# Attention's blocks in the order q, k, z, v, with probabilities turned through memory

## The reference, cut to what matters

```
h = RMSNorm(x);  proj = h @ w_in
attention:  12 heads x 128, three dilated windows mixed:
            s = q k^T / sqrt(128) + log_count      (log_count: -1e30 where no window holds the pair)
            p = exp(s - max s);  o = (p v / sum p) * silu(z)
conv:       o = b * conv3(c * u) * silu(z)         retention: o = norm(decayed (q k^T) v) * silu(z)
merged = sum over the branches of sigmoid(g) * (o @ w_branch)
x = x + RMSNorm(merged @ w_out)
```

## Time and profile before

| | |
|---|---|
| median of 3 runs | 2713.33 us (2712.95 to 2714.37) |
| the profiled execution's own time | 2712.87 us |
| its span (first to last instruction) | 2711.0 us |
| TensorE busy | 2699.1 us, 12120 matmuls |
| VectorE busy | 1881.8 us |
| ScalarE busy | 1308.4 us |
| mean granted TensorE clock | 0.999 |
| DMA | 579.43 MB, mean 214 GB/s |
| L1269 on VectorE (`w_trail`) | 1045 x 1223 ns = 1265.2 us |
| L1002 on ScalarE (`w_lead`) | 1045 x 1060 ns = 1101.7 us |
| L1566 on VectorE (turn of the probabilities) | 96 x 569 ns = 54.6 us |

### The profile page before, as it was taken

How to read it: one execution, slowest core, us unless ns; L and a number is a source line. 1 busy time by engine, 2 the same in 40 slices (tenths; PEclk the granted TensorE clock), 3 DMA queues, 4 the chain that set the end, 5 groups by cost and what they waited for, 6 DMA issues and landing times.

```text
span 2711.0 us, 30218 instructions
## 1 busy us (share of the span) xinstructions
PE 2699.1 (100%) x12120; PEld 2240.9 (83%) x12120; DVE 1881.8 (69%) x2102; ACT 1308.4 (48%) x1504; POOL 29.4 (1%) x42
## 2 busy tenths in 40 slices
PE   9999999999999999999999999999999999999998
PEld 7888888888888888888878888888888888888887
DVE  6656775888865666678576567658888656666884
ACT  6454554555543344454454545545555433444543
POOL 0000000000000000000000000000000000000000
PEclk9999999999999999999999999999999999999999
DMA  9677466665666676656576674657656656766563
GB/s 333 212 226 232 163 229 198 230 203 192 228 233 197 206 241 209 217 207 222 178 235 206 217 241 155 235 185 233 226 189 221 234 191 215 233 214 218 202 222 120
DMA packets 299291, 579.43 MB, mean 214 GB/s; under 512 B 12304, under 2 KB 37264, under 8 KB 298896
## 3 DMA queue, kind: packets, MB, share of 16 engines
q1 hardware_dynamic: 260976, 517.50, 56.9%
q10 hardware_dynamic: 37168, 55.13, 7.0%
q0 software_dynamic: 1008, 4.87, 0.5%
HBM read 548.10 MB, written 29.36 MB: 213 GB/s over the span
## 4 chain that ended last, share of the span: by engine, by line
PE 98%; DMA 1%; SPq 1%; DVE 0%; ACT 0%; issue 0%; POOL 0%; DVEq 0%; POOLq 0%
PE ps L928 29%; PE ps L930 29%; PE ps L929 29%; PE ps L895 3%; PE ps L894 3%; PE ps L893 3%; DMA raw<-w_in 0%; SPq L734 0%; PE ps L839 0%; PE ps L837 0%; PE ps L836 0%; PE ps L815 0%; PE ps L819 0%; DMA merged<-xT 0%; PE ps L801 0%; PE ps L820 0%
## 5 line engine op out<-in xcount | busy, mean ns | idle before, releaser
L1269 DVE TENSOR_TENSOR w_trail<-raw,w_lead 128x1024 fp32r<-128x1024 f32 x1045 | 1265.2, 1223 | 770.4 <-ACT w_lead L1002 767.3
L1002 ACT ACTIVATE w_lead<-raw 128x1024 fp32r<-128x1024 f32 x1045 | 1101.7, 1060 | 1250.0 <-PE ps L930 1120.7
L928 PE MATMUL ps<-w_lead,hT_lead 128*128 128x512 f32 x2944 | 1149.4, 390 | 2.1 <-DVE w_trail L1612 1.0
L930 PE MATMUL ps<-w_lead,hT_trail 128*128 128x512 f32 x2944 | 1145.6, 389 | 0.0
L929 PE MATMUL ps<-w_trail,hT_lead 128*128 128x512 f32 x2944 | 1145.5, 389 | 0.0
L928 PEld LDWEIGHTS ps<-w_lead,hT_lead 128*128 128x128 f32 x2944 | 552.7, 188 | 118.1 <-issue 3.6
L930 PEld LDWEIGHTS ps<-w_lead,hT_trail 128*128 128x128 f32 x2944 | 552.6, 188 | 115.0
L929 PEld LDWEIGHTS ps<-w_trail,hT_lead 128*128 128x128 f32 x2944 | 552.8, 188 | 113.5
L928 PE MATMUL ps<-w_lead,oT_lead 128*128 128x512 f32 x576 | 224.2, 389 | 0.0
L930 PE MATMUL ps<-w_lead,oT_trail 128*128 128x512 f32 x576 | 224.1, 389 | 0.0
L929 PE MATMUL ps<-w_trail,oT_lead 128*128 128x512 f32 x576 | 224.1, 389 | 0.0
(11 more groups left out here) (130 smaller groups left out, 1158.9 us busy)
## 6 DMA issues: line engine op xcount, KB each, us to landing
raw<-w_in SPq DMA_DIRECT2D x381, 1024.0 KB, 5.2
raw<-w_out SPq DMA_DIRECT2D x32, 1024.0 KB, 5.1
raw<-w_branch_a SPq DMA_DIRECT2D x24, 1024.0 KB, 5.2
raw<-w_branch_c SPq DMA_DIRECT2D x24, 1024.0 KB, 5.2
raw<-w_branch_r SPq DMA_DIRECT2D x24, 1024.0 KB, 5.4
bounce_q<-vq_sb ACTq DMA_DIRECT2D x18, 512.0 KB, 3.5
vq_sb<-bounce_q ACTq DMA_DIRECT2D x72, 128.0 KB, 4.1
bounce_z<-z_sb ACTq DMA_DIRECT2D x18, 512.0 KB, 4.0
```

What stands on the lines that cost most here:

```text
L928: pe.matmul(acc, lead[:, k, tok(t)], wl, start=opens, stop=False)
L930: last = pe.matmul(acc, trail[:, k, tok(t)], wl, start=False, stop=closes)
L1002: act.activation(w_lead[:, (l * HALVES + h) % SPLIT_SLOTS, :], raw[:, SLOT_OF[l, i][0], part:part + HALF * COLS], ACT.Copy).then_inc(lead_ ...
L1269: dve.tensor_tensor(w_trail[:, s, :], raw[:, SLOT_OF[l, i][0], part:part + HALF * COLS], w_lead[:, s, :].bitcast(F32), ALU.subtract).then_ ...
```

## The change

The order of attention's blocks becomes q, k, z, v. The places in the tables are now counted from attention's third block of a group (z, half 16 of the group). The table entries of attention, in halves from the group's start, are:

| step | before | after |
|---|---|---|
| q, k away (index) | 19, 27 | 18, 20 |
| q, k back (index) | 21, 29 | 20, 22 |
| q, k turned on VectorE (index) | 24, 32 | 23, 24 |
| scores on TensorE (after half) | 32 | 21 |
| scores on VectorE (index) | 36 | 25 |
| exp (index) | 37 | 26, in two parts |
| z leaves the accumulator (index) | 35 | 27 |
| probabilities | turned from index 39 in six pieces | away at 26, back at 29 and 30, turned at 31 and 32 |
| values on TensorE (after half) | 43 | 37 |
| z away, back, turned (index) | 48, 52, 58 | 42, 44, 47 |
| out, ScalarE and VectorE (index) | 59, 59 | 47, 48 |

`exp` writes its result into the tile `gates` (free at that time), already cut into quarters, in two parts of two heads; each part (384 KB) goes to HBM with one DMA and comes back with four, on ScalarE's queue, and VectorE turns it with two transposes of 128x384. The maxima are taken for two heads at a time. `PAIRS` stays as it was, so the branches for paired q and k (`q_scale`, `k_scale`, `scaled`) do nothing. In the diff:

```
-ROLES = {"attention": "vqkz", ...
+ROLES = {"attention": "qkzv", ...
+COUNTED_FROM = {"attention": 2, "conv": 0, "retention": 0}
 PE_DUE:
-    "attention": [("scores", 4 * B), ("values", 5 * B + 3)],
+    "attention": [("scores", 5), ("values", 2 * B + 4.5)],
 ACT_DUE:
-    "attention": [("q_away", 2 * B - 1), ("q_back", 2 * B + 1), ("k_away", 3 * B - 1), ("k_back", 3 * B + 1),
-                  ("exp", 4 * B + 1), ("z_away", 5 * B + 4), ("z_back", 6 * B + 4), ("out", 6 * B + 6.5)],
+    "attention": [("q_scale", -2), ("q_away", -2), ("q_back", 0), ("k_scale", 0), ("k_away", 0), ("k_back", 2),
+                  ("exp0", 6), ("p0_away", 6), ("exp1", 6), ("p1_away", 6), ("p0_back", 9), ("p1_back", 10),
+                  ("z_away", 2 * B + 6), ("z_back", 2 * B + 8), ("out", 2 * B + 11)],
 DVE_DUE:
-    "attention": [("q", 2 * B + 4), ("k", 3 * B + 4), ("scores", 4 * B), ("sums", 4 * B + 2)]
-                 + pieces("probs", 4 * B + 3) + [("values", 5 * B + 3), ("z", 6 * B + 6), ("out", 6 * B + 7)],
+    "attention": [("q", 3), ("k", 4), ("scores", 5), ("sums", 7), ("p0", 11), ("p1", 12),
+                  ("values", 2 * B + 4.5), ("z", 2 * B + 10.5), ("out", 2 * B + 12)],
...
-VALUES_LATE = 4      (v's block no longer leaves four halves late)
...
+        spare = gates[:, 0, 0:HPB * 3 * P].rearrange("p (s c) -> p s c", s=2)
...
+                if what in ("p0", "p1"):
+                    part = int(what[1])
+                    act.wait_ge(exp_ready, HPB * (l * GROUPS + g) + HPB // 2 * (part + 1))
+                    act.dma_start(bounce[what], spare[:, part]).then_inc(away[what], 16)
...
+                elif what in ("exp0", "exp1"):
...
+                    act.wait_ge(neg_max_ready, 2 * (l * GROUPS + g) + part + 1)
+                    by_quarter = spare[:, part].rearrange("p (j h c a) -> p h c j a", j=QUADS, h=HPB // 2, c=3)
...
-            def turn(l, what, mixer, g, piece):
-                src, dst, done = probs, probsT, probs_turned
-                for n in range(a, b):          (16 transposes of 32x384, in six pieces)
+            def turn(l, what, mixer, g):
+                dve.wait_ge(back[what], 16 * QUADS * trips(l, what, mixer, g))
+                squares = spare[:, part].rearrange("p (i h c a) -> p h c i a", i=QUADS, h=HPB // 2, c=3)
+                for h in range(HPB // 2):
+                    last = dve.transpose(probsT[:, HPB // 2 * part + h, :].rearrange("p (c i b) -> p c i b", c=3, i=QUADS),
+                                         squares[:, h])
```

More of the change, by code:

```diff
@@ L500, in build @@
         conv_joined = sem("conv_joined")
-        away = {what: sem(what + "_away") for what in ("q", "k", "z")}
-        back = {what: sem(what + "_back") for what in ("q", "k", "z")}
+        away = {what: sem(what + "_away") for what in ("q", "k", "z", "p0", "p1")}
+        back = {what: sem(what + "_back") for what in ("q", "k", "z", "p0", "p1")}
+        q_scaled = sem("q_scaled")
+        k_scaled = sem("k_scaled")
         q_turned = sem("q_turned")
@@ L1120, in side_work @@
                     bring_back(l, what[:-5], mixer, g)
[L1121 to L1124, removed]
+                elif what in ("q_scale", "k_scale"):
+                    n = role_block(mixer, what[0], g)
+                    if n in PAIR_OF:
+                        tile, done = {"q": (q_sb, q_scaled), "k": (k_sb, k_scaled)}[what[0]]
+                        act.wait_ge(*moved_out(l, n))
+                        for t in range(TILES):
+                            act.activation(quads(tile, t), quads(tile, t), ACT.Copy,
+                                           scale=x_rstd[:, t:t + 1]).then_inc(done, 1)
+                elif what in ("exp0", "exp1"):
+                    part = int(what[-1])
+                    if l > 0 and g == 0 and part == 0:
+                        act.wait_ge(residual_out, l * (16 * OUT_BLOCKS))
+                    act.wait_ge(neg_max_ready, 2 * (l * GROUPS + g) + part + 1)
+                    by_quarter = spare[:, part].rearrange("p (j h c a) -> p h c j a", j=QUADS, h=HPB // 2, c=3)
+                    for h in range(HPB // 2 * part, HPB // 2 * (part + 1)):
+                        for t, tiles in ((0, slice(0, 1)), (1, slice(1, 3))):
                             c = TILES * h + t
-                            last = act.activation(probs[:, h, cols], probs[:, h, cols], ACT.Exp,
+                            taken = probs[:, h, tiles.start * P:tiles.stop * P]
+                            last = act.activation(by_quarter[:, h % (HPB // 2), tiles],
+                                                  taken.rearrange("p (c j a) -> p c j a", j=QUADS, a=SQ), ACT.Exp,
                                                   bias=neg_max[:, c:c + 1], accum_out=row_sum[:, c:c + 1])
@@ L1434, in side_work @@
                         dve.wait_ge(*step_ready(l, s))
[L1435 to L1438, removed]
+                        if mixer != "attention":
                             dve.tensor_tensor(probsT[:, h, :], side(l, s)[:, 0:3 * P], const("causal"),
                                               ALU.mult).then_inc(drained[bank_no(l, s)], 1)
[L1441 to L1447, removed]
+                            continue
+                        dve.scalar_tensor_tensor(probs[:, h, :], side(l, s)[:, 0:3 * P], P ** -0.5,
+                                                 const("log_count"), ALU.mult, ALU.add).then_inc(drained[bank_no(l, s)], 1)
+                        if h % 2:
+                            two = slice(h - 1, h + 1)
+                            for i in range(h - 1, h + 1):
+                                dve.wait_ge(*step_drained(l, STEP["scores", mixer, g, i]))
+                            by_tile = neg_max.rearrange("p (h t) -> p h t", t=TILES)
+                            dve.tensor_reduce(by_tile[:, two, 0], probs[:, two, 0:P], AX_X, ALU.max, negate=True)
+                            dve.tensor_reduce(by_tile[:, two, 1], probs[:, two, P:3 * P], AX_X, ALU.max,
+                                              negate=True).then_inc(neg_max_ready, 1)
                 elif what == "sums":
```

71 lines of the change are left out of this document (38 added, 33 removed).

## The result

| | before | after |
|---|---|---|
| median | 2713.58 us (4 runs) | 2756.8 us (4 runs, 2755.43 to 2759.82) |
| ratio | | 1.0161, 95% interval 1.0143 to 1.0178 |
| span of the profiled execution | 2711.0 us | 2755.9 us |
| mean granted TensorE clock | 0.999 | 0.991 |

The account below looks back on a forecast made before the run. TensorE, 98% of the chain, was taken as the bound. k's turn and trip 15.3 us plus exp beside z 1.2 us made 16.5 us on 2712.87, 2729.4, as a median 2729.8 us; range 2719 to 2744.

Parts of the forecast that it names:

- What bounds the kernel, and where the wait would appear: TensorE bounds the kernel, its busy time stays at 2699 us, and a gap appears ahead of the scores in six groups.
- The bare turn: Before the scores, TensorE waits 1.30 us for k's turn in each of six groups: 7.8 us; as sole-cost rival, 0.15.
- The trip of k: Before the scores, k's late DMAs push its turn; waits including the bare turn: 7.6 + 4.7 + 3.0 = 15.3 us.
- clock of index 24: Time scale in us with 0 at ScalarE's split at index 24; scores wanted at 2.24, k's turn ending at 3.54 at best.
- the late landing, -1.7: Second and third groups, before k's reads: k away lands at most 7.1 us after issue, at -1.7 on the clock of index 24.
- the trips decide: Rival, before the scores: k away lands at the late bound, 24.4 us plus 6 for exp and z, 30.4 us, 2743.7; chance 0.12.
- the -6.0: Second and third groups: k away alone lands in 2.8 us, at -6.0 on the clock of index 24.
- The clock: Rival: TensorE's clock falls after waits, first groups only at risk, some 8 us on top, 2738; chance 0.09.
- sign of being wrong: For the whole kernel, the prediction would be wrong if the granted clock is below 0.99.
- Exp beside z: At indices 26 to 28, exp ahead of z leaves a tenth of cover: 0.2 us x 6 = 1.2 us, bounds 0 and 6.
- Edits at nothing: VectorE's fewer turns, the probabilities' trip, z's turn with out, and v's and the values' places: zero, together within 2 us.

Follow-up runs that it names:

- scores later: The changed kernel with the scores and all that follows up to the turn of the probabilities four halves later: 2714.2 us, ratio 1.0007.
- trip alone: The kernel before with old block order and places, but exp in two parts and the probabilities turned through memory in two parts: 2713.29 us, ratio 1.0002.
- k ahead of q's reads: The changed kernel with k away issued before q back on ScalarE's queue, both still at index 20: 2743.53 us, ratio 1.0115.
- only q's trip earlier: The changed kernel with q away at 17 and back at 19, k staying at 20 and 22: 2745.52 us, ratio 1.0123.
- filled gap: The changed kernel with matmuls whose results nobody reads put ahead of the wait for q's and k's turn before the scores: 2744.05 us, ratio 1.0114.
- scores one half later: The changed kernel with the scores and all that follows up to the turn of the probabilities one half later: 2739.49 us, ratio 1.0098.
- all trips earlier: The changed kernel with q away at 17, k away then q back at 19, k back at 21: 2724.14 us, ratio 1.0042.
- both one index on: The changed kernel with q away 18, back 20, k away 21, back 23, one index later than in only q's trip earlier: 2771.28 us (1 run).

## Why the prediction was wrong, step by step

- **What bounds the kernel, and where the wait would appear.** Right in the place, not in the size. TensorE was the bound, and all six waits that matter stand ahead of the scores. That TensorE's busy time would stay at 2699 was wrong: it was 2716.0, by the clock (below). VectorE's 42.2 us less (41 were forecast) brought nothing in three kernels (after, scores later, trip alone).
- **The bare turn.** Forecast 1.30 us a group. With the trips out of the way four groups have 1.17 or 1.18; the six together 8.1 for 7.8. Right.
- **The trip of k: the step that failed.** Its term with the bare turn was 15.3 us, measured 29.1. The second and third groups were given 1.9 us each (bounds 1.3 and 3.1) and waited 4.02, 3.85, 3.96 and 4.97; the first groups were given 4.7 and 3.0 (late bounds 7 and 5) and waited 6.99 and 5.32. The issue times were right: the send was to be issued by -8.8 on the clock of index 24, whose time 0 would have been 169.12 - 2.72 + 0.48 = 166.9, and it was issued at 158.16 - 166.9 = -8.7. Two things were wrong.
  - The landing of the send. Some 4.4 us was taken, as for q's reads, with 2.8 and 7.1 named as bounds; it took 7.4 to 7.6 us in the second and third groups and 6.0 and 6.1 in the first. The 2.8 of the earlier trace rows is a median over attention and retention: retention's six sends of k took 2.6 us, attention's own 2.9 to 3.5. And the late landing, -1.7, was named but never carried on: the 3.1 us come from a send seen at -4.5 and slow reads (7.1 us), and the rival "the trips decide" takes 3.1 x 4 for the late bound all the same.
  - The path. I had only the reads' landing in the sum of these groups. What ended last was the chain behind the wait on ScalarE's queue: the reads' issue, a split, a trail, q's turn, a trail, k's turn. I had written that chain for the first group of layer 0 alone. With a landing after 7.1 us it gives 3.9 us a group (-1.7 + 1.8 + 1.1 + 1.1 + 1.3 + 1.2 + 1.3 - 2.24). In the second group the scores' weights were wanted at 169.1 and the chain ended at 173.27. By the reads alone, there at 170.8 (3.9 on that clock), the wait would have been 3.0 us. So of the 2.1 us that this group's wait was over 1.9, about 1.1 are the send's late landing, net of reads that were faster than the 6.0 us taken, and 1.0 the chain. This division is read from the trace; no run takes the splits out from behind the reads.
- **The Trainium skill's rule that forbade the -6.0.** I had it in the text (the Trainium skill, DMA: Bandwidth & Descriptors, section Queues, rings and completion order: a completion signal lands only behind the earlier writes of the same DMA engine, whatever queue they came from) and said that the sum was the same with or without it. In after the order was as it says: the last of q's reads landed 6.3 us after the send's issue, the send after 7.4. By the runs the delay comes from loads on another queue too: in the kernel with k ahead of q's reads the send issued 0.39 us behind a load landed at 157.1, the load itself 7.0 us after 149.80, at 156.8. That agrees with the rule. But in the kernel with only q's trip earlier the send was seen at 162.3 and the load issued 0.39 us ahead of it at 163.1, so a send does not wait for the whole of such a load.
- **The clock.** This rival had 0.09 and 8 us, with "nothing" for waits under 3 us. It came in all six groups and cost 12.75 us by the filled gap (15.5 by the counting of starts). The mistake was to give it a chance of its own: it hangs on the length of the gap, so each microsecond of the trips' error moved it too, and with it all six groups were at risk and not the first ones only. Half of the time waited, the rival's rule for the size, gives 14.6 us for the gaps as measured, near the total, but not group by group: 2.75 us more behind 6.99, 2.69 behind 3.85. The rival "the trips decide" (30.4 us) together with the measured 12.75 would be 43, but by luck: of its 30.4 us 6 are for exp and z, which cost nothing, and 24.4 for the trips, which cost 29.1. As a sign of being wrong, a mean clock below 0.99 was too coarse: it was 0.991.
- **Exp beside z.** 1.2 us forecast, 0 measured: no gap at half 27 or 28. The working was close. On the clock of index 26 (split at 181.80, second group of after) split 27 started at 7.0 (7.0 forecast), z was done at 11.4 (11.4), and half 28's trail, started at 193.40, was done at 12.8 (13.0 for its split); TensorE came to half 28 at 195.14, 13.3 (13.1). Some 0.5 us of cover were left, where a tenth was worked out. In the kernel with the scores one half later exp and z's eviction meet at one index, and five groups lose 1.3 us each.
- **Edits at nothing.** Nothing, by two runs (2714.2 with the change but for the scores' place, 2713.29 with the probabilities' trip alone; their intervals reach 4.3 and 3.0 us). Their reads took 5.3 us to land and ended 2.0 us of VectorE's idle time.

## What to carry to other kernels

A transfer's price is that of its place: read what was issued just ahead of it on every queue and has not landed, and if no row shows such a case, carry the loaded bound through the whole sum. When an engine's queue waits for a transfer, carry the delay through everything queued behind it before the next step, not only through the transfer. And price a wait of TensorE together with the clock: here a wait up to 2.3 us cost only itself, and one from 3.8 us on 1.5 to 2.75 us more.

## What the runs showed of the hardware

How long TensorE was idle ahead of the scores, and what its next work took (first score to second matmul behind the scores, 2.93 us at full clock), over 30 gaps of five kernels (after, k ahead of q's reads, scores one half later, all trips earlier, only q's trip earlier):

| gap | clock stayed | clock fell | extra time when it fell |
|---|---|---|---|
| 1.1 to 2.3 us | 12 | 0 | |
| 2.4 to 3.3 us | 1 (3.25) | 3 (2.47, 2.92, 3.14) | 1.6 to 1.7 us |
| 3.8 us and more | 0 | 14 | 1.5 to 2.75 us |

The same length did not always give the same outcome, so I can name only these bounds. The six gaps of both one index on, 4.7 to 10.4 us, all lowered the clock too. The stretch of the scores behind a gap of 4.17 us, in the kernel with k ahead of q's reads, shows the price in another way: (1 - 0.88) x 14 = 1.68 us, and by the starts it is 4.60 - 2.93 = 1.67.

```profile
168.00:182.00 14.00, 14.00 (x60) 11.74 (x59) 6.00 (x10) 6.08 (x19) 0.00 (x0) 0.88 0.31 104
```

The Trainium skill (TensorE: Matmul & The Clock Gate, section on the HAM clock gate) has an idle engine dropped to half rate and released by activity; the 0.50 in the stretches of after, which ended while TensorE was working, agrees. A second surprise: a transpose of 128x384 took 554 ns and one of 32x384 569, so it is the columns that cost, and four times as many partitions are free.
